# A decoder step in float32: the last latent tile with k outermost, and the queries' input normalised in fours

## The reference, cut to what matters

```python
def shared_latent_kv(x, pos, g_in, w_down, g_latent):
    ckv, kpe = jnp.split(rms_norm(x, g_in) @ w_down, [KV_LORA_RANK], axis=-1)
    return rms_norm(ckv, g_latent), rope(kpe, pos)

def modulated_prenorm(x, c, w_ada, b_ada, g_pre):
    mod = (jax.nn.silu(c) @ w_ada + b_ada)[:, None, :]
    shift, scale, gate = jnp.split(mod, 3, axis=-1)
    return rms_norm(x, g_pre) * (1 + scale) + shift, gate

def mla_queries(h, pos, w_in, g_q, w_uq, w_kv_up):
    qa, z = jnp.split(h @ w_in, [Q_LORA_RANK], axis=-1)
    q = (rms_norm(qa, g_q) @ w_uq).reshape(b, t, N_HEADS, QK_NOPE_DIM + QK_ROPE_DIM)
    ...
```

## Time and profile before

| what | value |
| --- | --- |
| median of 3 runs | 2170.14 us (2169.33 to 2173.61) |
| profiled execution | 2168.84 us, of which the span from first to last instruction is 2167.0 |
| TensorE busy | 2051.3 us, 95% of the span, 16136 matmuls |
| VectorE busy | 1273.7 us, 59% |
| ScalarE busy | 775.6 us, 36% |
| GpSimd busy | 222.4 us, 10% |
| mean granted clock of TensorE | 0.972 of full speed |
| bytes read from memory | 342.45 MB at 171 GB/s over the span |

### The profile page before, as it was taken

How to read it: one execution, slowest core, us unless ns; L and a number is a source line. 1 busy time by engine, 2 the same in 40 slices (tenths; PEclk the granted TensorE clock), 3 DMA queues, 4 the chain that set the end, 5 groups by cost and what they waited for, 6 DMA issues and landing times.

```text
span 2167.0 us, 42020 instructions
## 1 busy us (share of the span) xinstructions
PE 2051.3 (95%) x16136; PEld 1889.3 (87%) x16136; DVE 1273.7 (59%) x1906; ACT 775.6 (36%) x1162; POOL 222.4 (10%) x103
## 2 busy tenths in 40 slices
PE   6889999999999999999978999999999989989995
PEld 5689999999999999999978899998888855569995
DVE  2687677777777777887767620313444332229776
ACT  3243333333333333545444432223445321114542
POOL 0100000000000000000023233333122200001001
PEclk9899999999999999999989899999999999999997
DMA  9955665565555565634553122234221367742447
GB/s 370 403 173 185 208 212 189 196 212 199 203 186 188 200 210 203 232 120 138 172 204 151 64 71 85 102 123 161 78 84 56 105 188 225 238 151 79 130 159 207
DMA packets 133470, 371.58 MB, mean 171 GB/s; under 512 B 13379, under 2 KB 40899, under 8 KB 131075
## 3 DMA queue, kind: packets, MB, share of 16 engines
q1 hardware_dynamic: 132226, 367.93, 49.9%
q0 software_dynamic: 1152, 2.36, 0.6%
HBM read 342.45 MB, written 27.79 MB: 171 GB/s over the span
## 4 chain that ended last, share of the span: by engine, by line
PE 82%; DVE 7%; DMA 5%; issue 3%; SPq 2%; ACT 1%; ACTq 0%; DVEq 0%
PE ps L778 30%; PE ps L782 15%; PE ps L712 8%; PE ps L719 4%; PE ps L751 3%; PE ps L1072 2%; PE ps L1041 2%; PE ps L1056 2%; PE ps L1170 2%; PE ps L1201 2%; PE ps L1129 2%; DMA ada_first_ring<-adastream 1%; DMA s<-adastream 1%; PE ps L868 1%; PE ps L737 1%
## 5 line engine op out<-in xcount | busy, mean ns | idle before, releaser
L674 POOL TENSOR_TENSOR w_lo<-w_raw,w_hi 128x1024 fp32r<-128x1024 f32 (+1 forms) x91 | 215.1, 2364 | 1750.8 <-ACT w_hi L1253 1750.8
L1309 ACT ACTIVATE w_hi<-w_raw 128x1024 fp32r<-128x1024 f32 x180 | 190.6, 1059 | 338.8 <-PE ps L782 184.5
L1762 DVE TENSOR_TENSOR w_lo<-w_raw,w_hi 128x1024 fp32r<-128x1024 f32 x184 | 225.3, 1224 | 121.6 <-ACT w_hi L1309 118.2
L778 PE MATMUL ps<-operand_hi,w_hi 128*128 128x288 f32 x1080 | 290.0, 295 | 0.0
L778 PE MATMUL ps<-operand_lo,w_hi 128*128 128x288 f32 x1080 | 289.7, 294 | 0.0
L778 PE MATMUL ps<-t_hi,w_hi 128*128 128x288 f32 x992 | 272.9, 301 | 4.9 <-DVE c_v L1893 2.8
L778 PE MATMUL ps<-t_lo,w_hi 128*128 128x288 f32 x992 | 267.7, 296 | 0.0
L712 PE MATMUL ps<-operand_hi,w_hi 128*128 128x288 f32 (+1 forms) x704 | 193.5, 303 | 14.2 <-DVE operand_lo L1721 11.8
L778 PEld LDWEIGHTS ps<-operand_hi,w_hi 128*128 128x128 f32 x1080 | 202.7, 188 | 0.1
L778 PEld LDWEIGHTS ps<-operand_lo,w_hi 128*128 128x128 f32 x1080 | 202.7, 188 | 0.0
L1253 ACT ACTIVATE w_hi<-w_raw 128x1024 fp32r<-128x1024 f32 (+1 forms) x91 | 92.8, 1020 | 304.2 <-PE ps L719 191.6
(11 more groups left out here) (318 smaller groups left out, 3879.6 us busy)
## 6 DMA issues: line engine op xcount, KB each, us to landing
w_raw<-wstream SPq DMA_DIRECT2D x177, 512.0 KB, 3.4
ada_ring<-adastream SPq DMA_DIRECT2D x114, 512.0 KB, 4.7
a<-wstream SPq DMA_DIRECT2D x90, 512.0 KB, 4.6
s<-wstream SPq DMA_DIRECT2D x45, 512.0 KB, 3.2
ada_first_ring<-adastream SPq DMA_DIRECT2D x36, 512.0 KB, 9.4
ada_third<-adastream SPq DMA_DIRECT2D x32, 512.0 KB, 6.3
page_t<-pages SPq DMA_DIRECT2D x48, 320.0 KB, 3.3
page_latent<-pages SPq DMA_DIRECT2D x56, 256.0 KB, 3.0
```

The lines of the kernel that those rows point to most:

```text
L674: pool.tensor_tensor(WL[:, n.slot, 0:width], WR[:, n.slot, 0:width], WH[:, n.slot, 0:width].bitcast(F32), ALU.subtract).then_inc(w_lo_read ...
L778: pe.matmul(PS[:, bank, 0:HALF], WH[:, c.slot, k * P:(k + 1) * P], x(k), start=(first and k == 0 and x is hi), stop=False, skip_group_chec ...
L1309: act.activation(WH[:, c.slot, :], raw, ACT.Copy).then_inc(w_hi_ready, 1)
L1762: dve.tensor_tensor(WL[:, c.slot, :], raw, WH[:, c.slot, :].bitcast(F32), ALU.subtract).then_inc(w_lo_ready, 1)
```

## The change

Four things change, on three engines.

- TensorE runs the rope key's tile with k outermost: for each k and half, high x high, high x low and low x high follow each other. The last matmul of each k raises a new semaphore, `xg_read`. The sums of the latent's squares move from ahead of the first query tile to behind the second.
- VectorE makes `h1` in four groups of four tiles (`HG`), each by one product of 128x2304 and two instructions on 4x64 sample elements. The low parts of all 16 tiles follow at once, and only then the fourth latent tile, the squares' sums and the rope key.
- ScalarE runs the prompt parts in fours, and rounds a group into `operand_hi` one group behind, each tile as soon as `xg_read` says that the rope tile has read its k. The squares come behind the weight rounding of the first query tile's second chunk. The root for the latent comes behind the first two query tiles.
- The loops over the two rounds of query tiles on TensorE and ScalarE are written out.

```diff
-            tile(Chunk(W_KV + W_THREE + 2), 2, cols=ROPE, split=1)
-            column_sums([kv_sq_used], CT)
-
-
-            with pe.Fori(0, CT // 2) as i:
+            n = Chunk(W_KV + W_THREE + 2)
+            pe.wait_ge(w_hi_ready, n.at(1))
+            pe.wait_ge(w_lo_ready, n.at(1))
+            for k in range(KT):
+                for a in range(2):
+                    for w, x in ((WH, OH), (WH, OL), (WL, OH)):
+                        last = pe.matmul(PS[0:ROPE, 4 + a, 0:HALF], w[:, n.slot, k * ROPE:(k + 1) * ROPE],
+                                         x[:, k * T + a * HALF:k * T + (a + 1) * HALF],
+                                         start=(k == 0 and w is WH and x is OH), stop=(k == KT - 1 and w is WL))
+                last.then_inc(xg_read if k < KT - 1 else w_used, 1)
+
+
+            for i in range(CT // 2):
                 for j in range(2):
                     pe.wait_ge(qa_evac[j], i + BEGUN)
-                    tile(Chunk(W_MLA + 2 * j, 4, i), j, ready=h1_ready if j == 0 else None)
+                    tile(Chunk(W_MLA + 4 * i + 2 * j), j, ready=h1_ready if i == j == 0 else None)
+                if i == 0:
+                    column_sums([kv_sq_used], CT)
...
+            def h1_high(q):
+
+                act.wait_ge(h1_raw, q + 1)
+                for k in range(HG * q, HG * q + HG):
+                    act.wait_ge(h1_prompt_done, k + 1)
+                    if k < KT - 1:
+                        act.wait_ge(xg_read, k + 1)
+                    else:
+                        act.wait_ge(w_used, W_MLA)
+                    act.activation(OH[:, k * T:(k + 1) * T], B1[:, k * T:(k + 1) * T], ACT.Copy).then_inc(h1_hi, 1)
+
+            round_w(Chunk(W_KV + W_THREE + 1))
+            round_w(Chunk(W_KV + W_THREE + 2))
+            h1_prompt(0)
+            round_w(Chunk(W_MLA))
+            h1_prompt(1)
+            h1_high(0)
+            h1_prompt(2)
+            h1_high(1)
+            h1_prompt(3)
+            h1_high(2)
+            h1_high(3)
+            round_w(Chunk(W_MLA + 1))
...
-            with act.Fori(0, CT // 2) as i:
-                n = Chunk(W_MLA + 2, 4, i)
+            for i in range(CT // 2):
+                n = Chunk(W_MLA + 2 + 4 * i)
                 for j in range(2):
                     round_w(n + 2 * j)
                     round_w(n + (2 * j + 1))
+                    if i == 0:
+                        act.wait_ge(kv_sq_used, CT - 1 + j + BEGUN)
                     act.wait_ge(qa_sq_used[j], i + BEGUN)
                     act.activation(halves(TT[j][:, :]), pair(j), ACT.Square).then_inc(qa_sq[j], 1)
...
+                if i == 0:
+                    root(3, 4)
...
+            def h1(q):
+
+                tiles = B1[:, HG * q * T:HG * (q + 1) * T].rearrange("p (k n) -> p k n", n=T)
+                x = X[:, HG * q * T:HG * (q + 1) * T].rearrange("p (k n) -> p k n", n=T)
+                dve.tensor_tensor(tiles, x, R0[:, :].unsqueeze(1).broadcast_to([P, HG, T]), ALU.mult).then_inc(h1_normed, 1)
...
+            for q in range(KT // HG):
+                h1(q)
+            for k in range(KT):
+                rest(k, h1_hi, k + 1, h1_ready)
+            latent(3)
+            for t in range(CT):
+                latent_square(t)
```

More of the change, by code:

```diff
@@ L60 @@
 ADA0 = 2 * KT // AT4
-AHEAD = 4
+HG = 4
 W_THREE = KT // 2
@@ L339, in build @@
         h1_raw, h1_hi, h1_ready = sem("h1_raw"), sem("h1_hi"), sem("h1_ready")
+        xg_read = sem("xg_read")
         ckv_ready, kpe_ready = sem("ckv_ready"), sem("kpe_ready")
@@ L1489, in _, with h1_prompt @@
             root(2, 3)
-            def h1_prompt(tiles):
-                for k in tiles:
-                    act.wait_ge(h1_normed, k + 1)
+            def h1_prompt(q):
+                act.wait_ge(h1_normed, q + 1)
+                for k in range(HG * q, HG * q + HG):
                     h = B1[:, k * T:k * T + TP]
                     act.activation(h, h, ACT.Identity, bias=MOD[:, 48 + k, 0:1], scale=AT[:, k, 0:1]).then_inc(h1_prompt_done, 1)
+            def h1_high(q):
+                act.wait_ge(h1_raw, q + 1)
+                for k in range(HG * q, HG * q + HG):
+                    act.wait_ge(h1_prompt_done, k + 1)
[16 more added lines that the diff above has]
+            round_w(Chunk(W_MLA + 1))
             for t in range(CT):
-                if t < 3:
-                    round_w(Chunk(W_KV + W_THREE + 1 + t))
                 act.wait_ge(kv_evac, t + 1)
@@ L1504, in _ @@
                 act.activation(TT[t % 2][:, :], CKV[:, t * T:(t + 1) * T], ACT.Square).then_inc(kv_sq, 1)
[L1505 to L1516, removed]
             act.wait_ge(x_parked, 16)
-            act.wait_ge(h1_raw, KT)
-            with act.Fori(0, CT // 2) as i:
-                n = Chunk(W_MLA + 2, 4, i)
+            for i in range(CT // 2):
+                n = Chunk(W_MLA + 2 + 4 * i)
                 for j in range(2):
@@ L1523, in _ @@
                     round_w(n + (2 * j + 1))
+                    if i == 0:
+                        act.wait_ge(kv_sq_used, CT - 1 + j + BEGUN)
                     act.wait_ge(qa_sq_used[j], i + BEGUN)
                     act.activation(halves(TT[j][:, :]), pair(j), ACT.Square).then_inc(qa_sq[j], 1)
-                    act.activation(halves(QA[:, bass.ds(i * (2 * T) + j * T, T)]), pair(j), ACT.Copy).then_inc(qa_evac[j], 1)
+                    act.activation(halves(QA[:, (2 * i + j) * T:(2 * i + j + 1) * T]), pair(j), ACT.Copy).then_inc(qa_evac[j], 1)
+                if i == 0:
+                    root(3, 4)
             def gate_tiles(i, n, between=None):
@@ L2121, in _, with mine @@
                 latent(t)
[L2123 to L2137, removed]
+            def h1(q):
+                tiles = B1[:, HG * q * T:HG * (q + 1) * T].rearrange("p (k n) -> p k n", n=T)
+                x = X[:, HG * q * T:HG * (q + 1) * T].rearrange("p (k n) -> p k n", n=T)
+                dve.tensor_tensor(tiles, x, R0[:, :].unsqueeze(1).broadcast_to([P, HG, T]), ALU.mult).then_inc(h1_normed, 1)
+                dve.wait_ge(h1_normed, q + 1)
+                samples = tiles[:, :, TP:T].rearrange("p k (b t) -> p k b t", b=NB)
+                def mine(table, k0):
+                    return table[:, k0 + HG * q:k0 + HG * (q + 1), 1:NM].unsqueeze(3).broadcast_to([P, HG, NB, NS])
+                step(dve.tensor_tensor(samples, samples, mine(AT, 0), ALU.mult))
+                dve.tensor_tensor(samples, samples, mine(MOD, 48), ALU.add).then_inc(h1_raw, 1)
+            for q in range(KT // HG):
[5 more added lines that the diff above has]
+                latent_square(t)
             dve.wait_ge(w_used, W_MLA)
@@ L2141, in _ @@
             dve.wait_ge(kv_evac, CT + 1)
[L2142 to L2145, removed]
             rstd(3, R, 4)
```

## The result

The changed kernel takes 2154.12 us (median of five runs, 2153.03 to 2160.72) against 2171.08 us of the kernel before (median of five: the three runs known before and two more, 2169.33 to 2176.85). The ratio is 0.9926, with an interval of 0.9907 to 0.9944, which is 12 to 20 us less. The profiled execution takes 2153.03 us, its span 2151.2.

What follows compares the result with a forecast made beforehand. TensorE bounds the kernel, busy 95%, waiting longest for operand_lo. Its 17.37 us excess falls to 1.9 (0.7 + 0.2, 0.97 later), saving 15.45: 2168.84 to 2153.4, or 2154.7 on the median's footing; forecast 2153 to 2156.5, range 2150 to 2159.

Steps and rivals of the forecast that it cites:

- The rope tile: TensorE's rope tile with k outermost: still 96 matmuls in 12.8 us, 0 change (bounds 0 to 0.5), k freed one by one.
- VectorE's timeline: h1 groups at 3.35 us against 4.8 for four singles; first low part ready 1180.0, 16th 1190.1, ahead of TensorE's need.
- ScalarE's timeline: Prompt parts and roundings without slack until 1188.3, then the second chunk's weight rounding; TensorE waits 0.7 us for it.
- The second query tile's rounding: ScalarE's weight rounding behind the latent's squares, 1194.6 to 1195.7; TensorE's wait for it 0 to 0.6 us, 0.2 taken.
- The sums: Sums of the latent's squares, moved behind the second projection tile: 0.97 us to the next matmul at full clock.
- The first query square's sum: VectorE's first addition of the query squares, expected at about 1228; cover 4 us, cost 0.
- The gap: TensorE's 2.36 us "issue" ahead of the first gate tile: a wait for copies, left with its slow clock, 0 saved.
- Rival (b): The gap ahead of the gates goes with the loops, 2.36 plus 1.7 us of slow clock: 2150.6 us; chance 0.05.
- Rival (a): Larger new stalls in the first query tile and a lowered clock, 2 to 4.5 us more: 2157 to 2159; chance 0.11.
- Rival (c): VectorE's 128x2304 product with a repeated operand is slow; at three times 2.55 us the kernel takes 2172.6; chance 0.02.
- Rival (d): Little change: low parts still pace the first tile, products needing 1.5 to 2.5 times as long; 2160 to 2170; chance 0.04.
- the new 0.7 us wait: TensorE between the first query tile's chunks, 1188.67 to about 1189.4, for a weight rounding ScalarE does after high 3.

Runs made afterwards that it cites:

- e5_rope_alone: The kernel before with only the rope tile's matmuls in the new order, nothing waiting for single k: 2173.63 us (1 run), first gate matmul at 84.26 us.
- e8_late3: The changed kernel with twelve useless 128x576 products on VectorE between the last h1 group and the first low part: 2167.25 us (1 run), gate at 79.00.
- e1_gap: The changed kernel with the first gate tile waiting only for the copy of its own two banks: 2149.27 us, ratio 0.9907 to the kernel before.
- e10_unrolled: The kernel before with the two loops over query tiles written out on TensorE and ScalarE, nothing else: 2168.39 us (1 run).
- e8_late1: The changed kernel with four useless 128x576 products on VectorE between the last h1 group and the first low part: 2156.11 us (1 run), gate at 70.85.
- e2_round: The changed kernel with ScalarE rounding the first query tile's second weight chunk ahead of the last four roundings into operand_hi: 2153.26 us, ratio 0.9928 to the kernel before.
- e0_after: The changed kernel measured again without edit: 2155.94 us, ratio 0.9928 to the kernel before, first gate matmul at 68.19 us.
- e4_rope_undone: The changed kernel with the rope tile's matmuls back in the old order: 2160.0 us (1 run), first gate matmul at 75.81 us.
- e6_sums_ahead: The changed kernel with the sums of the latent's squares back ahead of the first query tile: 2165.79 us (1 run), gate at 82.97.
- e7_singles: The changed kernel with VectorE making h1 in 16 single tiles instead of four groups: 2159.24 us (1 run), gate at 73.06.

## Why the prediction was right

The forecast was 2154.7 and the median is 2154.12; 15.45 us were to be saved in the stage and 15.65 were. (17.37 less 0.7, 0.2 and 0.97 is 15.50; the 15.45 of the forecast is off by 0.05.) That the two medians agree within 0.6 us is in part luck: the five runs spread over 7.7 us, and the medians of the two kernels lie 16.96 apart, of which the stage explains 15.65. The prediction stands on the stage. Step by step, with 1.02 us taken off the times of the new trace:

- **The rope tile** was to run 12.8 us in any order: the first query matmul comes 12.64 us behind its start, with no pause (e5_rope_alone shows the order to be free). The 0.16 us are not gained; TensorE waits that much longer for the rounding.
- **VectorE's timeline**: groups done at 1179.3, measured 1179.05; the 16th low part at 1190.1, measured 1189.85; a small instruction 0.42, measured 0.43. The hold of 4.7 us and GpSimd's wait behind the third product came as worked out. The lead of 2.3 us over the tile was 2.25 (e8_late3).
- **ScalarE's timeline**: the second chunk's rounding from 1188.3, measured 1188.31. The wait for it, 0.7, is recorded with 0.72; by starts it is 0.89 (1190.42 where the pace gives 1189.53).
- **The second query tile's rounding**: 0 to 0.6 of wait, 0.2 taken. The rounding started at 1194.21 where 1194.6 was worked out, and the wait was 0; the first tile's second chunk took 6.51 us (1190.42 to 1196.93) in place of 6.40. The whole tile took 13.80, 1.0 us above its 12.80, where 0.9 stood.
- **The sums** took 0.97 us. **The first query square's sum** was expected at 1228 and came at 1225.6: GpSimd held that chain once and not twice, so the cover was wider than 4 us.
- **The gap** ahead of the gates stayed, 2.27 us, and so did the slow clock behind it (6.05 us for 32 matmuls). The first was worked out. The second was left as it was without a reason, and that it stayed is luck worth 1.6 us: in five of the other kernels the same pause was followed by full clock (below). Rival (b) was rejected for the right reason, by e1_gap and e10_unrolled.
- **Rival (a)**, larger new stalls: they did not come, but e8_late1 shows how near they were: 3.1 us more on VectorE cost 2.6.
- **Rival (c)**: the product with an operand repeated over the middle dimension takes 2.55 us, as a contiguous one does. **Rival (d)**, products that need 1.5 to 2.5 times as long, falls with it.

What the prediction did not see is that its parts are conditions of one chain and not contributions. It never split the gain, and the working by one timeline is what carried it. The weak place was the remark that the new 0.7 us wait stems from ScalarE's order: true, but e2_round shows that a mere exchange moves it.

## What to carry to other kernels

Where three engines hand tiles round, write down one absolute timeline of all three with the durations of their rows and put the lock between VectorE and GpSimd in it; such a timeline was right to 0.4 us in the steps that TensorE waited for, up to the second query tile here, and 2.4 us too late at the query squares, where nothing hung on it. Before giving a wait a name, look at what ended 0.1 us ahead of the waiting instruction: "issue" was a wait for the copy of two banks that the next tile did not use, and naming it right was worth 4 us for two moved lines. When one engine's list has no slack, an instruction taken forward only moves the wait, until all that blocks behind it is moved as well.

## What the runs showed of the hardware

**The same pause, two clocks.** The pause ahead of the gates was followed by a lowered clock in the kernel before (2.36 us). With 2.27 us it was followed by one in the changed kernel, e0_after, e8_late1 and e8_late3, and not in e2_round, e4_rope_undone, e6_sums_ahead, e7_singles and e10_unrolled. From the first gate matmul to the second sums it is 27.2 us in the first four and 25.6 to 25.7 in the other five. The rows are the three microseconds from the first gate matmul on, first in the changed kernel and then in e2_round; the granted clock is 0.56 and 1.00.

```profile
1238.71:1241.71 3.00, 3.00 (x14) 3.00 (x15) 1.87 (x1) 0.00 (x0) 1.26 (x1) 0.56 0.19 35
```

```profile
1240.92:1243.92 3.00, 3.00 (x22) 3.00 (x23) 1.88 (x1) 0.00 (x0) 1.27 (x1) 1.00 0.18 48
```

It was the same in both profiles of the changed kernel. So a pause of this length cost 2.3 or 3.9 us, and kernels that differ only elsewhere in the stage fell on either side. The cause was not settled.

**GpSimd does not always get its turn.** In e8_late1 its instruction is recorded from 1190.13 with 5.73 us for 2.4 of work. By that length it got in at about 1193.5. VectorE ran its 16 low parts without a break in that time; its next instruction, at 1193.53, read PSUM:

```profile
1190.13 5.73 POOL L675 TENSOR_TENSOR w_lo<-w_raw,w_hi 128x1024 fp32r<-128x1024 f32 x1 [14.52 <-ACT w_hi L1264]
```

```profile
1182.83 10.79 DVE L1744 TENSOR_TENSOR operand_lo<-tiles,operand_hi 128x576 fp32r<-128x576 f32 x16
1193.53 0.76 DVE L2135 TENSOR_TENSOR latent<-ps,rstd 128x576 f32<-128x576 f32 x1
```

In the instruction of 1213.85 in the earlier trace rows it was let in after about 0.25 us, in the changed kernel right behind the third product, and in e8_late3, among the same low parts, after 0.3 us (2.70 recorded). What decides this was not settled. The Trainium skill, "SBUF — State Buffer", section "SBUF: two separate sides", has the shared pair held for a whole instruction, and the changed kernel's trace agrees; but here GpSimd was kept out for about five instructions in a row (3.3 us at 0.67 each). In this kernel it made a wait of 0.41 us of TensorE's for `w_lo`.
